# Where a block's experts wait for their weights and for the room of their results

## What is computed

```
h2  = rmsnorm(x) * (1 + sc2) + sh2                # 1024 tokens x 1024
e   = the top 2 of 8 experts in the token's top 1 of 4 groups    # 32 experts
ys  = (silu(xb @ w_gate[e]) * (xb @ w_up[e])) @ w_down[e]        # 1024 -> 512 -> 1024
out = rmsnorm(x + gt2 * sum(gate * ys))
```

## Time and profile before

| | |
|---|---|
| median of three runs | 1218.05 us |
| the profiled execution | 1220.27 us |
| its span, first to last instruction | 1218.4 us |
| mean granted TensorE clock | 0.990 |
| TensorE busy | 1165.2 us (96%) |
| VectorE, ScalarE, GpSimd busy | 557.7, 279.3, 262.0 us |
| HBM read, written | 310.18 MB, 35.14 MB |

### The profile page before, as it was taken

The page is one execution under the profiler, slowest core; times in us unless marked ns, Lnnn a source line. Parts: engine busy times, 40 slices in busy tenths (PEclk is TensorE's granted clock), DMA queues, the critical chain, the costliest instruction groups (busy, mean ns, idle before and its releaser), DMA issues.

```text
span 1218.4 us, 31527 instructions
## 1 busy us (share of the span) xinstructions
PE 1165.2 (96%) x13908; PEld 930.8 (76%) x13908; DVE 557.7 (46%) x1043; ACT 279.3 (23%) x561; POOL 262.0 (21%) x330
## 2 busy tenths in 40 slices
PE   4799999999999999999988999999999999999996
PEld 1799988888888878788876777888778798766663
DVE  1765554342287888866683222222222222223227
ACT  3842211211265666633220000000000000000004
POOL 0000000000210000100004443543545535333210
PEclk9899999999999999999999999999999999999998
DMA  9639854444376777371069999999999999999938
GB/s 378 269 144 324 297 172 133 152 130 152 111 250 229 169 171 150 103 245 42 36 233 386 412 413 413 414 415 412 413 413 412 413 413 413 408 412 411 394 131 347
DMA packets 96844, 345.33 MB, mean 283 GB/s; under 512 B 18483, under 2 KB 47011, under 8 KB 69059
## 3 DMA queue, kind: packets, MB, share of 16 engines
q1 hardware_dynamic: 75795, 312.04, 67.7%
q10 hardware_dynamic: 11696, 14.44, 4.1%
q0 software_dynamic: 9216, 16.82, 3.7%
HBM read 310.18 MB, written 35.14 MB: 283 GB/s over the span
## 4 chain that ended last, share of the span: by engine, by line
PE 44%; DMA 6%; SPq 4%; DVE 2%; issue 1%; POOL 0%; ACT 0%; DVEq 0%; POOLq 0%
PE p_layers L2264 23%; PE p_layers L2279 11%; SPq L2053 4%; PE p_y L2076 3%; DMA raw<-in_w_up 2%; DMA slot<-in_w_up 2%; PE p_y L2078 2%; PE p_y L2077 2%; PE p_layers L2456 1%; DMA raw<-y_rows 1%; PE p_turn L1805 1%; PE p_turn L1815 1%; DMA arena<-h_rows,arena 0%; DVE arena L1735 0%; DVE x L2509 0%
## 5 line engine op out<-in xcount | busy, mean ns | idle before, releaser
L1899 POOL DMA_INDIRECT arena<-h_rows,arena x96 | 98.9, 1030 | 169.0 <-PE p_layers L2264 139.7
L2264 PE MATMUL p_layers<-slot,xt 128*32 128x256 f32 x2208 | 130.3, 380 | 0.4
L2191 ACT ACTIVATE arena<-p_layers 128x384 f32<-128x384 f32 x32 | 15.7, 492 | 497.8 <-PE p_layers L2264 497.8
L2213 DVE TENSOR_TENSOR arena<-arena,p_layers 128x384 f32<-128x384 f32 x32 | 17.7, 554 | 239.2 <-ACT arena L2191 239.2
L2141 POOL DMA_INDIRECT y_rows<-arena x96 | 95.7, 997 | 129.9 <-DVE arena L2230 109.7
L2264 PEld LDWEIGHTS p_layers<-slot,xt 128*32 128x32 f32 x2208 | 95.6, 110 | 30.7 <-issue 5.8
L2076 PE MATMUL p_a<-tokens_high,half_high 128*128 128x512 f32 (+1 forms) x272 | 101.8, 374 | 0.2 <-DVE half_low L705 0.2
L2077 PE MATMUL p_a<-tokens_low,half_high 128*128 128x512 f32 (+1 forms) x272 | 100.9, 371 | 0.0
L2078 PE MATMUL p_a<-tokens_high,half_low 128*128 128x512 f32 (+1 forms) x272 | 100.8, 371 | 0.0
L2264 PE MATMUL p_layers<-raw,xt 128*32 128x256 f32 x1632 | 97.4, 380 | 2.5 <-DMA raw<-in_w_up 1.3
L2230 DVE TENSOR_TENSOR arena<-p_layers,gate_slices 128x256 f32<-128x256 f32 x96 | 40.5, 421 | 110.1 <-PE p_layers L2279 98.6
(11 more groups left out here) (392 smaller groups left out, 2232.4 us busy)
## 6 DMA issues: line engine op xcount, KB each, us to landing
slot<-in_w_down SPq DMA_DIRECT2D x26, 1024.0 KB
raw<-in_w_ada SPq DMA_DIRECT2D x24, 1024.0 KB, 8.0
slot<-in_w_gate SPq DMA_DIRECT2D x23, 1024.0 KB
slot<-in_w_up SPq DMA_DIRECT2D x23, 1024.0 KB
raw<-in_w_gate SPq DMA_DIRECT2D x17, 1024.0 KB
raw<-in_w_up SPq DMA_DIRECT2D x17, 1024.0 KB
ahead<-in_w_gate SPq DMA_DIRECT2D x16, 1024.0 KB
ahead<-in_w_up SPq DMA_DIRECT2D x16, 1024.0 KB
```

Source lines behind the costliest of these rows:

```text
L1899: pool.indirect_dma_start(s.xg[n % 2][:, b * SLICE:(b + 1) * SLICE], None, slices, bass.IndirectOffsetOnAxis(ap=s.token[:, b, n:n + 1], ax ...
L2264: last = pe.matmul(gate_up[quad(g), b, :, :], x.xt[n % 2][:, k, b, :], weights[:, :, r, g * ES:(g + 1) * ES], start=(k == 0), stop=(k == K ...
```

## The change

Two waits move. In `first_layer` the waits for both parts stand ahead of the first matmul; the loop over the parts is otherwise the same. In `second_layer` the wait for all three blocks of the results before becomes one wait in each block's loop: block b of expert n asks for `y_ok` of 3(n-1) + b + 1, so for block b of expert n-1.

```diff
@@ -2256,6 +2256,8 @@
                 for c in range(2):
                     i = place[n, c]
                     pe.wait_ge(loaded[i % SLOTS], 32 * (i // SLOTS + 1))
+                for c in range(2):
+                    i = place[n, c]
                     weights = x.slots[i % SLOTS].rearrange("p (w r e) -> p w r e", w=2, r=4)
                     for r in range(4):
                         k = 4 * c + r
@@ -2269,11 +2271,11 @@
 
                 i = place[n, 2]
                 pe.wait_ge(h_turned, n + 1)
-                if n >= 1:
-                    pe.wait_ge(y_ok, BLOCKS * n)
                 pe.wait_ge(loaded[i % SLOTS], 32 * (i // SLOTS + 1))
                 weights = x.slots[i % SLOTS].rearrange("p (k n) -> p k n", k=KE)
                 for b in range(BLOCKS):
+                    if n >= 1:
+                        pe.wait_ge(y_ok, BLOCKS * (n - 1) + b + 1)
                     for k in range(KE):
                         for g in range(GROUPS):
                             last = pe.matmul(sums[quad(g), b, :], x.ht[n % 2][:, k, b, :], weights[:, k, g * SLICE:(g + 1) * SLICE],
```

## The result

Twenty runs each: **1222.84 us** after (1219.76 to 1227.34), 1218.42 us before (1216.64 to 1220.45). The ratio is 1.0035, 95% interval 1.0027 to 1.0042, or +4.3 us (+3.3 to +5.1). The prediction was 1221.7 us, slower, with a range of 1219.2 to 1223.6.

What follows compares the result with a forecast made beforehand. Late in the expert stage TensorE runs at the weights' pace, so work behind the last `in_w_up` landing decides. 5.49 - 1.67 + 0.1 - 0.4 + 0.2 = +3.7 us on 1218.05 gives 1221.7 us, range 1219.2 to 1223.6.

Steps and rivals of the forecast that it cites:

- What bounds the kernel: Late in the expert stage TensorE runs at the weights' pace; work behind the last `in_w_up` landing at 1158.56 us decides.
- The early wait: Expert 31's first layer starts only when its second part lands, delaying expert 30's second layer: +5.49 us.
- the onset: Waiting for both parts costs nothing up to about expert 17; from there first layers start later, by up to 5.35 us.
- The wait by block: Expert 31's second layer follows expert 30's directly, no longer waiting for VectorE's last block: -1.67 us.
- The scatters come closer: Behind the last second layer, GpSimd's closest spacing limits the scatters of experts 30 and 31: +0.2 us.
- S + 12.1: Last scatter's issue time, S being expert 30's second-layer start: S + 7.52 plus three scatters at 1.53 us spacing.
- 62 more waits: Two more TensorE waits in each of 31 second layers: between nothing and 0.4 us, taken as +0.1 us.
- The load lands earlier: Expert 29's scatter falls behind the last weight landing, freeing DMA time: 0 to -0.6 us, taken as -0.4.
- All shifts with it: Everything behind the last second layer moves by the same amount, except the scatters of experts 30 and 31.
- no starvation: Rival: unprofiled, TensorE doesn't wait for weights late in the stage, leaving only the -1.67: 1216.4 us, chance 0.07.
- an earlier landing: Rival: two experts' gather and scatter traffic leaves the last part's way, 2.5 us instead of 0.4: 1219.7 us, chance 0.15.
- the dry queue: Rival: later slot releases delay the loads, moving the last landing 2 us later: 1223.6 us, chance 0.08.

Runs made afterwards that it cites:

- kernels with added fillers: Before, waits by block at expert 31, other banks and after, each with 30 more unread matmuls ahead of the row sums: -1.2, -2.4, -1.9, +2.7 us against before.
- second edit alone: Kernel before with only the second layers' wait for the last results split by block: 1221.0 against 1219.38 us, +1.2 us.
- other banks: Kernel before with expert 31's second-layer results in other PSUM banks, asking only for expert 30's first piece: 1219.9 us, +0.4 us.
- first edit alone: Kernel before with only both parts of every first layer waited for ahead of its first matmul: 1224.64 against 1219.38 us, +5.2 us.

## Why the prediction was right, and where it was not

*What bounds the kernel.* Right. The landing of the last `in_w_up` sets the stage's end, it is where it was, and the trace's chain runs over it.

*The early wait, +5.49.* Right, for the reason given: +5.2 measured alone, 5.65 in the trace of after, 0.2 where TensorE isn't starved, 2.2 to 7.4 depending on which experts wait early. The rule of the Trainium skill ("DMA: Bandwidth & Descriptors", section "Rules for kernel authors", to wait late) agrees at the end of the stage. Where weights were in time, waiting early cost 0.2 us, which the runs can't tell from nothing. That the delay doesn't add up is right too: from 1036 us on six first layers wait, 6.9 us in all and 2.6 at most. One wait of 0.3 us for `in_w_up` before 1036 is new, so the onset, put at expert 17, was nearly nothing in size as well.

*The wait by block, -1.67.* Right as far as the layer: the last two second layers start 5.18 us apart instead of 6.85. What it was worth in the end was mis-sized, by the next term at least. The 1.67 us also had a part that the prediction did not see: 0.9 us of it is the late release of block 2, which is absent in the kernels with added fillers.

*The scatters come closer, +0.2.* It measured +0.96 in after and left -0.7 of -1.67 in the second edit alone. The formula S + 12.1 had the three pieces reach GpSimd in their order of time; block 1's release 1.5 us late was in no row that I read. Rows of before had such releases (777.35 and 874.89, at experts 6 and 12), with idle times behind that hid them. This is the term that the runs show to be mis-sized, by 0.8 us, in all four kernels that have the second edit or its like and no added fillers.

*62 more waits, +0.1.* Not contradicted, not separated. From the start of expert 30's second layer to the fillers behind expert 31's it is 10.71 us in after, 10.51 in after with added fillers, which has the same 62 waits, and 10.90 with other banks, which has no wait inside a layer. So nothing of it can be put down to the waits. The kernels with all 62 waits and with expert 31's alone are 0.7 us apart (+1.2 and +0.5), well within their intervals.

*The load lands earlier, -0.4.* Not seen in before and after. The landing comes 504.6 us after the first expert matmul both before (1158.56 - 653.94) and after (1158.96 - 654.38). But this figure varies by 1.1 us among the profiles, and 0.4 us can't be told from two. (The four with early waits at expert 30 and before it, after among them, average 504.9 us, the eight others 505.4, in ranges that overlap: that would fit the term and does not show it.) The queue did not run dry: SP's last issue was 0.34 us later.

*All shifts with it.* The weakest step. I took what lies behind the last second layer as rigid but for the scatters. It holds eight matmuls whose duration is not fixed: 3.5, 5.0 to 5.2 or 6.2 to 6.4 us in the kernels without added fillers, at granted clocks of 1.00, 0.72 and 0.50. In after they took 6.4 us and in before 5.2, and this is 1.2 of the 7.1 us between the two profiles. Whether the edits make it so is not shown. Two of the kernels with the second edit's effect read 6.2 and 6.4, but the second edit alone reads 5.0 and the first alone 5.2, and each is one execution. That with fillers the second edit is worth 0.7 to 1.2 us more than the fillers alone (-1.9 and -2.4 against -1.2) is a difference that the intervals don't separate from zero, and nearly all of it (0.8 us) stands in the traces ahead of the last scatter.

So the sum of +3.7 came within 0.6 us of +4.3, and part of that is luck. By the traces the scatters were 0.8 us too low, the landing's -0.4 didn't show, and the eight matmuls had 1.2 us more in the one execution of after: 2.4 us, where the medians leave room for 0.6. The first edit alone and the second alone (+5.2 and +1.2) also make more than both together. The intervals (-0.5 to +3.0 for the second alone) allow both, so how the last 2 us divide stays open. The two rivals that made it milder (no starvation, an earlier landing) fell with the waits and the landing; the dry queue, which would have reached 1223.6 with another mechanism, with SP's issues.

**Of what was to be seen**, the block of 192 in 10.7 us, the idle put down to `in_w_up`, expert 31's start within 1 us of 1158.2 (1159.09, 0.89 off), the missing 1.5 us of "issue", the end at 1179.6 (1169.45 + 2 x 5.18 = 1179.81) and the DMA share of 1.01 came true.

**A better version** is before with the wait by block at expert 31 and 30 more fillers ahead of the row sums: -2.4 us (-4.5 to -0.4), or with other banks -1.9. About half of it is the fillers' (-1.2 alone, an interval that holds zero), by the clock and by the earlier releases together. The first edit belongs in neither.

## What to carry to other kernels

Waiting for two loads at once costs the work that could have been done on the first, but only at the end of a chain that waits for loads; ask which load lands last and what work stands behind it. A gain of a microsecond at the end of one stage has to be followed through the next burst of matmuls, whose duration swung by up to 3 us here. To read such a swing from one profile of each kernel is not enough: one of four kernels with the second edit's effect didn't have it. Where a change's profile and its median disagree, add up the profile's difference piece by piece and see which pieces differ between executions of one kernel too. And when an experiment adds something to isolate one cause, look ahead of the place as well: the kernels with added fillers differed from the others 500 us before the first of these ran.

## What the runs showed of the hardware

- The granted clock can fall behind an idle stretch: after 6.54 us of waiting a part of a first layer ran at 0.53, 7.46 us instead of 5.18; after 1.4 us it took 5.18. The stretch of the row sums had 0.50 after waits of 3.48, 3.90 and 4.89 us, 0.72 after 2.77, 3.02, 3.20 and 3.49, and 1.00 after 2.82 and behind fillers without a wait. So the idle time just ahead does not settle it alone: 3.48 and 3.49 us gave different clocks, and so did 2.77 and 2.82. The Trainium skill ("TensorE: Matmul & The Clock Gate", Part 1) has the two levels and that idle time brings the lower; the traces agree.
- The release of a block of matmuls to VectorE can come late. Block 2 of a second layer was handed over 6.3 to 6.8 us after the layer's start in most layers of the kernels without added fillers, and at about 5.4 in those with them. Block 1 came at 5.5 to 6.2 us instead of 3.7 at experts 6 and 12 of every kernel without added fillers and, at 5.2, at expert 31 of those where also the pause was gone; in the four with fillers it came at 3.7 at all three. The profile calls the source of these late ones of block 1 "remote". The cause stays open.
- SP's issues of loads stand 29 us ahead of their landing, and that did not change (29.27 us before, 29.32 after) though TensorE took up expert 31's first part 6.0 us later.
